# A ring of expert weights refilled in another order: next gate and up first, then the last down

## The reference: what is computed

```python
for grp in range(N_GROUPS):
    act = jax.nn.silu(jnp.einsum('nd,edf->nef', x, wg[grp])) * jnp.einsum('nd,edf->nef', x, wu[grp])
    act = act * comb[:, grp, :, None].astype(act.dtype)
    y = y + jnp.einsum('nef,efd->nd', act, wd[grp]).astype(f32)
```

## Time and profile before

| | |
|---|---|
| median of 3 runs | 500.22 us (498.77 to 500.42) |
| the profiled execution | 499.25 us, span of its instructions 497.4 us |
| PE busy | 469.1 us, 94% of the span |
| VectorE, ScalarE, POOL busy | 282.3, 149.4, 37.3 us |
| DMA moved | 143.00 MB, mean 287 GB/s; q1 131.03 MB, q0 10.85 MB |

### The profile page before, as it was taken

One profiled execution on the slowest core, in us unless ns is written; L12 is line 12 of the kernel. 1 busy time (PEld: TensorE's weight loads), 2 busy tenths in 40 slices (PEclk: granted clock), 3 DMA queues, 4 the chain that ended last, 5 costly groups with the idle time before them and its releaser, 6 DMA issues.

```text
span 497.4 us, 10561 instructions
## 1 busy us (share of the span) xinstructions
PE 469.1 (94%) x4300; PEld 314.7 (63%) x4300; DVE 282.3 (57%) x695; ACT 149.4 (30%) x367; POOL 37.3 (8%) x45
## 2 busy tenths in 40 slices
PE   7999999999999999999999999989999999786793
PEld 5888898888786445575656655655665555445441
DVE  3888999999878965327474322333442222231266
ACT  3440238530257323420243221221222111120134
POOL 0000000000001000000012031011202111000000
PEclk9999999999999999999999999999999999986798
DMA  8991000000009999449967999999999999999984
GB/s 269 350 371 58 0 1 1 1 1 1 3 5 338 411 424 427 185 179 362 344 258 286 434 375 424 413 426 423 424 421 420 424 419 424 428 419 426 417 334 172
DMA packets 29089, 143.00 MB, mean 287 GB/s; under 512 B 4357, under 2 KB 11685, under 8 KB 20336
## 3 DMA queue, kind: packets, MB, share of 16 engines
q1 hardware_dynamic: 23360, 131.03, 65.6%
q0 software_dynamic: 5248, 10.85, 6.2%
q10 hardware_dynamic: 432, 0.44, 0.3%
HBM read 133.21 MB, written 16.78 MB: 302 GB/s over the span
## 4 chain that ended last, share of the span: by engine, by line
PE 58%; DMA 27%; DVE 6%; SPq 5%; issue 2%; ACT 1%; DVEq 0%; POOLq 0%
PE bank_pair L1564 12%; PE bank_pair L1765 9%; DMA area_x<-in_w_exp 8%; DMA area_g<-in_w_exp 8%; PE bank_pair L1890 7%; PE bank_pair L1574 4%; DMA area_w<-in_w_out 4%; DMA area_g<-expert_out 4%; PE bank_pair L1898 4%; PE bank_pair L1514 3%; PE bank_pair L1913 3%; SPq L516 3%; PE bank_pair L1702 3%; DVE area_m L930 2%; PE bank_pair L1921 2%; PE bank_pair L1883 2%
## 5 line engine op out<-in xcount | busy, mean ns | idle before, releaser
L1765 PE MATMUL bank_pair<-area_w,area_m 128*128 128x512 f32 x128 | 56.8, 595 | 0.3 <-DMA area_w<-in_w_out 0.3
L930 DVE SCALAR_TENSOR_TENSOR area_m<-area_g,cols,area_m 128x512 f32<-128x512 f32 x60 | 41.3, 744 | 0.0
L1765 PEld LDWEIGHTS bank_pair<-area_w,area_m 128*128 128x128 f32 x128 | 23.6, 190 | 27.0 <-issue 26.5
L1890 PE MATMUL bank_pair<-area_w,area_m 128*64 128x256 f32 x320 | 38.5, 383 | 0.9 <-DMA area_w<-in_w_exp 0.5
L1890 PE MATMUL bank_pair<-area_g,area_m 128*64 128x256 f32 x256 | 31.1, 385 | 1.8 <-DMA area_g<-in_w_exp 1.8
L1890 PEld LDWEIGHTS bank_pair<-area_w,area_m 128*64 128x64 f32 x320 | 22.4, 137 | 15.4 <-issue 5.3
L2114 DVE COPY cst<-bank_pair 128x128 f32<-128x128 f32 (+1 forms) x36 | 9.5, 264 | 34.5 <-PE bank_pair L1904 25.7
L2132 DVE COPY area_m<-bank_pair 64x512 f32<-64x512 f32 x20 | 13.9, 694 | 22.9 <-PE bank_pair L1913 22.9
L1890 PEld LDWEIGHTS bank_pair<-area_g,area_m 128*64 128x64 f32 x256 | 17.6, 136 | 13.4 <-issue 5.3
L1898 PE MATMUL bank_pair<-area_w,area_m 128*32 128x128 f32 x512 | 22.0, 324 | 3.4 <-DMA area_w<-in_w_exp 3.4
L2121 DVE TENSOR_TENSOR cst<-cst,bank_pair 128x128 f32<-128x128 f32 x22 | 6.4, 289 | 32.5 <-ACT cst L2035 31.0
(11 more groups left out here) (436 smaller groups left out, 868.5 us busy)
## 6 DMA issues: line engine op xcount, KB each, us to landing
area_g<-in_w_exp SPq DMA_DIRECT2D x14, 2048.0 KB
area_w<-in_w_exp SPq DMA_DIRECT2D x13, 2048.0 KB, 30.4
area_w<-in_w_exp SPq DMA_DIRECT2D x16, 1024.0 KB, 8.1
area_g<-in_w_exp SPq DMA_DIRECT2D x14, 1024.0 KB
area_x<-in_w_exp SPq DMA_DIRECT2D x4, 2048.0 KB, 25.1
area_w<-in_w_in SPq DMA_DIRECT2D x6, 1024.0 KB, 14.1
area_w<-in_w_out SPq DMA_DIRECT2D x2, 2048.0 KB, 15.1
expert_out<-area_g SPq DMA_DIRECT2D x2, 2048.0 KB, 22.7
```

What stands on the lines that cost most here:

```text
L930: ins = V.scalar_tensor_tensor(out=mixT[:, i, :], in0=src, scalar=w, in1=mixT[:, i, :], op0=ALU.mult, op1=ALU.add)
L1765: ins = T.matmul(bank[7][:, :], mixT[:, k, j * P:(j + 1) * P], w_out_sb[:, n, k, :], start=(k == 0), stop=(k == KT - 1))
L1890: ins = T.matmul(out_b[h * BC:(h + 1) * BC, 0:2 * P], x[:, k, :], w_gate_up[slot][:, :, k, h * P:(h + 1) * P], start=(k == 0), stop=(k == ...
```

## The change

In the refill loop of SP, the down weights of a step are no longer issued directly behind its gate and up weights, but behind the gate and up weights of the next step. The expert's number is read from the table once for each of the two transfers. The waits in front of each transfer are the same as before, each with its own transfer. The transfers, their sizes and their number stay.

```diff
         def experts_sync(sp):
             sp.wait_ge(d_fill, 32)
             sp.wait_ge(tables, 1)
+            def expert_at(s_):
+                e = sp.value_load(tab[0:1, 1 + MORE + USE[s_]:2 + MORE + USE[s_]], min_val=0, max_val=NE - 1)
+                return lambda w: w[bass.ds(e, 1)].rearrange("a p n -> (a p) n")
+
+            def down_again(s_):
+                of = expert_at(s_)
+                sp.wait_ge(dn_done, LAST_OF[s_ - RING] + 1)
+                load_down(sp, of, s_ % RING, d_dn[s_ % RING])
+
             for s_ in range(RING, NE):
-                slot = s_ % RING
-                e = sp.value_load(tab[0:1, 1 + MORE + USE[s_]:2 + MORE + USE[s_]], min_val=0, max_val=NE - 1)
-                of = lambda w: w[bass.ds(e, 1)].rearrange("a p n -> (a p) n")
+                of = expert_at(s_)
                 sp.wait_ge(gu_done, LAST_OF[s_ - RING] + 1)
-                load_gate_up(sp, of, slot, d_gu[slot])
-                sp.wait_ge(dn_done, LAST_OF[s_ - RING] + 1)
-                load_down(sp, of, slot, d_dn[slot])
+                load_gate_up(sp, of, s_ % RING, d_gu[s_ % RING])
+                if s_ > RING:
+                    down_again(s_ - 1)
+            down_again(NE - 1)
```

## The result

The changed kernel took 505.85 us (median of 4 runs, 504.93 to 507.0) against 500.32 for the kernel before (4 runs, 498.77 to 502.1): ratio 1.011, 95% interval 1.0078 to 1.0141. In a later session, 12 runs against 35 of before, it was 504.43 against 500.59: ratio 1.0062, interval 1.0035 to 1.0089, +3.1 us (1.7 to 4.5). Ratios and intervals are those on record; they are not quotients of the medians, which would give +3.8 us there. The forecast was +2.6 with a range of -0.2 to +4.6: the direction holds in both, the first result lies above the range, the second inside it.

What follows compares the result with a forecast made beforehand. The bytes left for the DMA engines at 422 GB/s were taken to set the end from about 300 us. The profiled execution's 499.25 + 1.1 (start) + 1.5 (tail) gave 501.85, on the median 502.8 us, range 500.0 to 504.8.

Steps and rivals of the forecast that it cites:

- What bounds the kernel: From about 300 us the bytes left over 422 GB/s set the end; earlier idle time of the DMA engines comes back.
- Part 1: Start of the refills: 1.9 us idle before gate/up 10, 0.8 us won elsewhere, net +1.1 us (+0.4 to +2.2).
- The sign that the prediction set: Next profile: a first read-back of expert rows anywhere but 1.1 us later than 477.06 would mean bytes don't set the end.
- Part 2: PE on the way, the loop to block 35: gate/up lands 2.5 us earlier, down 5.0 later; costs and gains nothing.
- Part 3: Last four blocks: down of block 38 waits for its load, PE's tail +2.95 us, the end +1.5 us (0 to +3.3).
- rival E: The clock stays down in the tail, or the early gap is larger: +1.1 + 3.3 and more, 504.6; chance 0.10.
- ScalarE's slack: At the end, PE was done 1.5 us before ScalarE's last square sum, so that much of PE's delay is absorbed.
- The sum: Whole kernel: 499.25 + 1.1 + 1.5 = 501.85 us for the profiled execution, 502.8 on the median.
- A: PE, not the DMA queue, is the path; gate/up landing 2.5 us earlier makes the kernel faster, 497.7; chance 0.08.
- B: Only the tail costs, SP's early loads cover the gap at the start: +1.5, 501.7; chance 0.12.
- C: Only the start costs, ScalarE's slack swallows the late down loads of the last four blocks: +1.1, 501.3; chance 0.16.
- D: Neither term: overlapping loads are served so evenly that order of issue isn't order of landing; 500.2; chance 0.08.

Runs made afterwards that it cites:

- middle_only: Kernel before, with the new order for the down weights of steps 13 to 26 alone; +0.35 us (-1.5 to +2.2), ratio 1.0007.
- start_only: Kernel before, with the new order for steps 7 to 12 alone, the old one from step 13; +1.0 us (-0.3 to +2.4), ratio 1.002.
- after_resid_first: Changed kernel, with the residual matmuls in front of the down product of block 38 instead of behind it; +0.45 us over before, ratio 1.0009.
- after: The changed kernel as first measured and profiled, against the kernel before; 505.85 us, ratio 1.011.
- after_again: The changed kernel once more, no edit, in a later session against the kernel before; 504.43 us, ratio 1.0062.
- tail_only: Kernel before, with the new order for the down weights of steps 27 to 30 alone; +2.5 us (+1.0 to +4.1), ratio 1.005.
- after_warm_long: Changed kernel, with 3 added matmuls before the down product of block 36 and 6 before those of 37 and 38; +1.8 us over before, ratio 1.0036.
- after_gate_first: Changed kernel, with gate and up of block b before down of block b-1 in PE's last four blocks; +0.9 us over before, ratio 1.0019.
- late_8_9: Kernel before, but down 8 behind gate/up 9 and down 9 behind gate/up 10; +2.1 us (+0.5 to +3.8), ratio 1.0043.

## Why the prediction was right or wrong

- **What bounds the kernel**: right. The stretch from 300 to 440 us is the same to the digit, 1.01 and 422 GB/s, middle_only costs nothing, and the early loss arrives at the rows read back.
- **Part 1, +1.1 us**: right in mechanism and within its bounds (+0.4 to +2.2), both of its parts somewhat smaller than forecast. The four moved issues came within 0.4 us of their forecast, the dip where it was put. One reading was short: the first packets of gate/up 7 are at 262.73 us, 0.99 us behind the issue; 0.86 is only where their slice of the row begins. The engines' idle time was 1.5 us in the dip (share 0.72 to 0.83 from F + 41 to 48 us in the seven traces with the new start, 0.99 to 1.02 in the four with the old one; forecast 1.9), and they won 0.56 us at F + 22 to 27 (0.88 to 0.94 against 0.74 to 0.86; forecast 0.5) and 0.1 behind the dip (forecast 0.3). Net it is 0.8 us by the shares and 1.0 by the bytes at F + 60 us. At the end, the 0.97 of start_only and the 1.07 of after_resid_first are the two traces of seven in which VectorE waited for the read-back. Over all seven against the four, the first pair of read-backs lands 0.4 us later and the last read-back 0.7 us, single traces -0.3 to +1.2. The sign that the prediction set, a first read-back 1.1 us later, failed in the changed kernel's own trace: counted from F it landed 0.3 us earlier (231.5 against 231.8). Landings scatter by as much as the effect, so that sign could not decide.
- **Part 2, nothing**: right as far as can be told, +0.35 within the noise and +0.2 in the trace.
- **Part 3, +1.5 us**: the right mechanism, mis-sized; it measured 3.1 (after, after_again, tail_only: S - W 22.94, 22.94, 22.89 against 19.83). The step that failed is "its 1.0 us, the residual matmuls L2321 of 1.98 us": I took the durations of the earlier trace rows, which are those of the full clock, for work that now stands behind a wait. From down of block 38 to block 39 it took 479.55 - 474.98 = 4.57 us, not 3.0, and since ScalarE's slack of 1.5 us was already spent, the 1.6 us went to the end in full. after_warm_long takes them back by keeping PE busy. The clock at half was the upper bound (+3.3) and rival E, at 0.10, but it was put on the wrong product: the bound let the product of block 39 take 3.64 us, and that one ran in 1.95 in both kernels, while the two groups ahead of it were slow. The bound's own sum, 1.5 + 1.69, is also 3.2 and not 3.3. For the forecast, showed 0.50 in the stretch where PE waited before, so the half clock behind the new wait deserved to be in it.
- **ScalarE's slack** of 1.5 us was right: of the 4.57 us by which block 39 moved against the landing, 3.11 arrived at the last square sum.
- **The sum.** By the changed kernel's two traces it is 3.6 and 4.3 us (0.4 and 1.2 up to W, 3.1 behind it); the 12 runs give 3.1 (1.7 to 4.5), the first 4 gave 5.5 (3.9 to 7.1). The mis-sized term alone, 3.1 in place of 1.5, gives 500.22 + 1.1 + 3.1 = 504.4, still inside the range (to 504.8); what carried the first result to 505.85 is the remaining 1.4 us, which the second session doesn't show again. It looks like chance: the first profile of before had one of the earliest F of the 13 (245.26), that of the changed kernel one of the latest. But only one of the four runs of each was profiled, so this isn't shown.
- **The rivals.** A (PE is the path, faster) falls with middle_only. B (only the tail) falls with the bytes at F + 60 us and start_only's R - F, though its time alone would not have told. C (the tail swallowed by slack) falls with tail_only, D with the order of the waits. Of E the first half came true in kind, the clock in the tail; a larger early gap did not.

## What to carry to other kernels

In a ring of loads through one queue, compare the order in which the last loads land with the order in which the consumer uses them; here two of the consumer's loops had different orders, and the new order of issue fitted only the first. Where it fitted, with the queue full, it gained nothing (middle_only), and making the last loop fit too left the trace 2.8 us late (after_gate_first). What took the tail's cost away was to put work that needs no load in front of the wait (after_resid_first). When a wait is moved in PE's stream, cost what stands behind it at the clock that the profile grants behind such a wait, not at the duration of the row before. At the start of a ring, a small load held back behind a large one whose buffer isn't free yet is missing from the queue meanwhile, here 1.05 MB or 2.5 us of transfers, and the queue can run dry for want of it. When single traces are compared, take several that should agree: here their landings differed by up to 0.9 us, once by more.

## What the runs showed of the hardware that was not expected

- A load queue doesn't stop at once: before the dip the rate fell from 287 to 0 GB/s over 1.6 us. The last load ahead of the dip (down 8) landed in sixteen parts between 290.2 and 292.3 us, so the engines ran dry one after another.
- A load has landed only with the last of its sixteen parts: for gate/up 31 the last part came 0.7 us behind the fifteenth in before and 3.2 us in late_8_9.
- The first expert product, 245 us into the kernel, came anywhere within 4.4 us over 13 executions of nearly the same mixer. That spread is larger than the effect studied, and only counting from it made single traces comparable. Its cause was not looked into.
